# Router and expert gathers on unnormalised token rows, turned rows first in a step, offset expert rows

## The chip, the cores and the metric

The kernel runs on one core of one Trainium2 chip. The metric is the device time of one launch in microseconds (us). The engines are PE (TensorE), DVE (VectorE), ACT (ScalarE), POOL (GpSimd) and SP (SyncE, which here only issues DMAs).

## The reference, cut to what matters

A first block (latent attention and a gated embedding) feeds a second one: gated delta rule and retention, an output product, and a mixture of 64 experts of which every token uses two. All is float32, with 1024 tokens of 1024 numbers. What the change touches is the end of the second block:

```python
x = x + jnp.einsum("bse,ed->bsd", mixed, w_out[l])
h2 = rms_norm(x, ffn_norm[l])          # x * rsqrt(mean(x*x) + EPS) * w
x = x + hierarchical_moe(h2, w_router_group[l], w_router_expert[l], w_gate[l], w_up[l], w_down[l])
...
g_logits = hf @ w_router_group         # 8 groups: the largest
e_logits = hf @ w_router_expert        # 64 experts: the best two of that group
xs = ht[tok]                           # token rows sorted by expert
gate = lax.ragged_dot(xs, w_gate, group_sizes)
up = lax.ragged_dot(xs, w_up, group_sizes)
y = lax.ragged_dot((jax.nn.silu(gate) * up).astype(xs.dtype), w_down, group_sizes)
```

## The kernel before

**The second block** handles 8 tiles of 128 tokens in steps. In step s the pieces named `n_` (new tile) work on tile s, `o_` (the states and outputs) on s - 1, `e_` (the output product, eight pieces `e_p0` to `e_p7`, and `e_x0`, `e_x1`, which add its two halves to the token rows `res`) on s - 2, `l_` (norm, turns, router logits) and `r_` (routing) on s - 3, `z_` (the expert table) on s - 4. The order of the pieces in a step is written out by hand in the list ORDER, with lists of their own in ENDING for steps T = 8, 9, 10 and 11; each engine runs the pieces that it has in that order. Steps 3 to 7 have all pieces and are alike. The eight PSUM banks are given out from the same lists: `n_` and `o_` jobs rotate over three banks each, the others have a home. H0 and H1 (the turned rows), M1 and OUT1 (the second half of the output product) live in bank 7, OUT0, M0, LG (logits), RK (rank) and TB (table) in bank 6; in the steps from T on H0 and H1 have banks 0 and 1. `begin` makes PE wait until the bank's last reader has let go of it.

For a tile, `l_sq` squares the rows on ACT (into `hn`, as a place to throw them), `l_rs` makes the scale on POOL, `l_hn` writes the normalised rows `hn` on DVE with a stride, `l_turn0` and `l_turn1` turn them on PE (four 128x128 blocks each) and copy them on ACT to `hn_t`, `l_logits` multiplies them with `w_r`, and ACT stores `hn` to `hn_d` in DRAM. `r_max` to `r_top2` choose experts on DVE (some twenty small operations from the first `r_one` to `r_m`), `r_rank` counts the tokens ahead in each expert on PE, `r_place` and `r_rows` work out the slots, `z_table` and `z_keep` sum them to a table, from whose last state `src_i`, the list for the gathers, is made. A piece named `q_` is the `r_` piece of the tile before. `x_10`, `x_40`, `x_48` are idle turns on PE that fill a wait.

**The experts** run in 32 pairs. A pair holds 128 slots, 64 for each of its two experts, filled from slot 0 of each half. POOL gathers the rows (`rows`, three buffers) by an indirect DMA from `hn_d`; PE turns them (`turn_rows`, L2890), ACT and DVE copy a half each (`half_rows`, L2962), PE makes the gate and up products (L2901), ACT and DVE silu and product, PE turns that and multiplies with the down weights (L2919), and POOL scatters the rows to `y_d`. The weights, 6.3 MB a pair, have three buffers and come on SP's queue. Pairs 0 to 2 are issued in the last steps; the gate and up weights of pair p + 3 when PE has made those products of pair p. At the end the token rows and the two rows of `y_d` of each token are added and normalised.

Of the kernel before, what the change touches and what calls it, by code (L numbers as in the profile page):

```python
# [32 lines left out]
N_BLOCKS = 2 * S // HB + EXPERTS - 1  # L33
# [6 lines left out]
for _name, _n in (("ident", P), ("tri", P), ("ones", P), ("inv", ROPE // 2), ("levels", 6 * HB), ("ident64", HB), ("decay", BH * P),  # L40
                  ("qdec", BH), ("kdec", BH), ("gend", BH), ("iota", P), ("neghalf", 8), ("before", P), ("asg", 2 * T), ("pcol", 1),
                  ("first", GROUPS), ("limit", EXPERTS)):
    CONST[_name] = (_at, _n)
    _at += _n
# [4 lines left out]
def constants():  # L49
# [27 lines left out]
    put("limit", HB + HB * (np.arange(EXPERTS)[None, :] % 2))  # L77
    ang = np.arange(S, dtype=np.float32)[:, None] * (10000.0 ** (-np.arange(0, HD, 2) / HD)).astype(np.float32)[None, :]
# [19 lines left out]
def build(nc, A, out):  # L98

    ctx = ExitStack()  # L100
    with ctx:  # L101
# [1838 lines left out]
        hn_d = dram("hn_d", (S, D))  # L1940
# [5 lines left out]
        ss_x4, ms_x4, rs_x4 = col(48, 1), col(49, 1), col(50, 1)  # L1946
# [5 lines left out]
        class Count:  # L1952
# [12 lines left out]
            def wait(self, eng, name, t):  # L1965
                if not isinstance(t, int) or t >= 0:
# [23 lines left out]
        ENDING = {T: ("l_sq o_read z_table z_keep o_turn l_rs o_new e_turn o_scores o_out l_hn e_p0 o_mix l_turn0 l_turn1 o_state o_sq e_p1 e_x0 "  # L1990
                      "l_logits e_p2 e_p3 r_max r_group o_end e_p4 e_p5 e_p6 e_p7 r_top1 r_top2 e_x1 r_rank r_place r_rows").split(),
                  T + 1: "e_turn l_sq l_rs z_table z_keep e_p0 l_hn e_p1 e_x0 e_p2 e_p3 e_p4 e_p5 e_p6 e_p7 e_x1 l_turn0 l_turn1 l_logits".split(),
                  T + 2: ("l_sq l_rs l_hn l_turn0 l_turn1 q_max q_group q_top1 q_top2 x_10 p_logits x_10 q_rank q_place q_rows z_table x_40 r_max z_keep r_group r_top1 r_top2 "
                          "r_rank x_10 r_place r_rows").split(),
                  T + 3: "z_table x_48 z_keep".split()}
        LAG = {"a": -1, "n": 0, "o": 1, "e": 2, "l": 3, "r": 3, "p": 3, "d": 3, "q": 4, "z": 4, "x": 4}
# [7 lines left out]
                  "e_p2": "OUT1", "l_turn0": "H0", "l_turn1": "H1", "l_logits": "LG", "p_logits": "LG", "r_rank": "RK", "q_rank": "RK", "z_table": "TB"}  # L2004
# [8 lines left out]
        for s in STEPS:  # L2013
            for name in ENDING.get(s, ORDER):
                t = s - LAG[name[0]]
                if 0 <= t < T:
                    for job in BEGINS.get(name, "").split():
                        if job in HOME:
                            b = HOME[job] if s < T else HOME_END[job] + (job == "LG" and t == T - 1)
# [39 lines left out]
        pool_l = Count("l_pool", "ms rs"); act_l = Count("l_act", "sq"); dve_l = Count("l_dve", "hn")  # L2059
# [4 lines left out]
        def d0_sp(sp):  # L2064
# [10 lines left out]
            sp.dma_start(fg_row[:, :], A["ffn_norm_2"][0].partition_broadcast(P)).then_inc(s_fg, 16)  # L2075
            sp.dma_start(w_r[:, :, 0:GROUPS], A["w_router_group_2"][0].rearrange("(p k) n -> p k n", p=P)).then_inc(s_wr, 16)
            sp.dma_start(w_r[:, :, GROUPS:], A["w_router_expert_2"][0].rearrange("(p k) n -> p k n", p=P)).then_inc(s_wr, 16)
            products_over(sp)
            load_tk(sp, 1)
            sp.dma_start(w_o2[:, :, :], A["w_out_2"][0].rearrange("(k p) n -> p k n", p=P)).then_inc(s_wo2, 16)  # L2080

# [1312 lines left out]
```

## Time and profile before

| | us |
|---|---|
| median of 3 runs | 2111.21 (2109.64 to 2113.0) |
| the profiled execution | 2114.67, its span 2112.9 |
| PE busy over the span | 1949.3 (92%), granted clock 0.969 |
| DVE, ACT, POOL busy | 794.8, 615.1, 600.9 |
| DMA moved | 371.80 MB, mean 176 GB/s |

The page gives shares over the whole span, in which many stages with different limits lie behind each other. The first block ends at about 1187 us, the steps of the second run to about 1565, the experts to about 2073, the closing sums to the end. In the page's 40 slices the DMA share is under 0.7 in every slice up to about 1585 and 0.9 or more in nearly all behind it.

### The profile page before, as it was taken

The page shows a single profiled execution, that of the slowest core. Times are in us where ns is not written, and L with a number is a line of the kernel's source. Part 1 is how long each engine was busy: PE and PEld are TensorE (multiplying, and loading weights), DVE is VectorE, ACT ScalarE, POOL GpSimd, SP SyncE. Part 2 cuts the span into 40 slices and gives each one's busy share as a digit, 9 for nine tenths or more (in the row PEclk, how much of TensorE's full clock was granted, in tenths as well). Part 3 has the DMA queues.
Part 4 walks back from the last instruction along what each step waited for, and adds up shares of the span by engine and source line. Part 5 has one row for each costly group of instructions (what it writes and reads, how often), then busy time and mean ns, then how long its engine had stood idle before and what let it go on. Part 6 is the DMA issues. An engine that isn't in the chain of part 4 may idle for free. (4 is left out here: it accounts for less than half of the span.)

```text
span 2112.9 us, 31128 instructions
## 1 busy us (share of the span) xinstructions
PE 1949.3 (92%) x12049; PEld 1376.3 (65%) x12049; DVE 794.8 (38%) x1445; ACT 615.1 (29%) x1324; POOL 600.9 (28%) x611
## 2 busy tenths in 40 slices
PE   8999999999999989999999899999979888878785
PEld 7998887787787766878887767677653223323222
DVE  5223246666453443441112356666531211111114
ACT  5233145555333442332122333232212111111111
POOL 1225387342120110001003576765211111111102
PEclk9999999999999999999999999999999999999998
DMA  5103461211320253622333422311669999999996
GB/s 209 52 31 139 137 214 27 51 26 46 140 92 21 50 111 67 91 60 86 104 105 106 165 76 81 100 62 56 244 247 420 424 425 424 424 424 422 420 389 271
DMA packets 101730, 371.80 MB, mean 176 GB/s; under 512 B 17429, under 2 KB 40154, under 8 KB 74714
## 3 DMA queue, kind: packets, MB, share of 16 engines
q1 hardware_dynamic: 82592, 323.55, 42.7%
q0 software_dynamic: 16704, 42.10, 5.1%
q10 hardware_dynamic: 2298, 4.23, 0.5%
q8 instruction: 98, 1.61, 0.3%
q14 instruction: 38, 0.31, 0.0%
HBM read 321.47 MB, written 65.14 MB: 183 GB/s over the span
## 5 line engine op out<-in xcount | busy, mean ns | idle before, releaser
L2901 PE MATMUL ps<-w_gu,rows_t 128*64 128x512 f32 x1024 | 257.8, 662 | 57.1 <-DMA w_gu<-w_up 55.5
L2901 PEld LDWEIGHTS ps<-w_gu,rows_t 128*64 128x64 f32 x1024 | 78.7, 151 | 212.9 <-issue 153.7
L3165 POOL DMA_INDIRECT y_d<-y_out,asg_i x32 | 32.1, 1003 | 426.5 <-DVE y_out L2985 400.5
L2976 DVE TENSOR_TENSOR act_s<-act_g,ps 128x256 f32<-128x256 f32 x32 | 13.5, 421 | 321.0 <-ACT act_g L2967 321.0
L2333 PE MATMUL ps<-w_o,mix_t 128*128 128x512 f32 x256 | 122.6, 609 | 0.0
L2919 PE MATMUL ps<-w_d,act_tt 128*64 128x512 f32 x512 | 116.9, 598 | 0.5 <-DMA w_d<-w_down 0.5
L1120 ACT ACTIVATE prob<-ps,stats 128x1024 f32<-128x1024 f32 (+7 forms) x128 | 94.4, 737 | 62.2 <-DVE stats L1083 61.8
L2967 ACT ACTIVATE act_g<-ps 128x256 f32<-128x256 f32 x32 | 12.3, 383 | 320.1 <-PE ps L2901 320.1
L310 PE MATMUL ps<-tk_lo,h_hi 128*128 128x512 f32 x256 | 100.4, 392 | 3.0 <-DVE tk_lo L302 3.0
L310 PE MATMUL ps<-tk_hi,h_hi 128*128 128x512 f32 x256 | 100.3, 392 | 0.0
L310 PE MATMUL ps<-tk_hi,h_lo 128*128 128x512 f32 x256 | 100.2, 391 | 0.0
L1083 DVE TENSOR_REDUCE stats<-ps 128x1 f32<-128x1024 f32 (+7 forms) x128 | 97.0, 758 | 4.4
L482 PE MATMUL ps<-w_u_lo,x_hi 128*128 128x444 f32 (+2 forms) x256 | 92.8, 363 | 5.6 <-DVE x_lo L302 3.6
L998 PE MATMUL ps<-consts,prob 128*128 128x128 f32 x576 | 89.3, 277 | 6.8 <-DVE prob_t L1057 5.4
L482 PE MATMUL ps<-w_u_hi,x_lo 128*128 128x444 f32 (+2 forms) x256 | 92.1, 360 | 0.0
L482 PE MATMUL ps<-w_u_hi,x_hi 128*128 128x444 f32 (+2 forms) x256 | 91.8, 359 | 0.0
L829 POOL TENSOR_SCALAR stats<-stats 128x1 f32<-128x1 f32 (+1 forms) x40 | 8.3, 207 | 278.1 <-ACT junk_b L1392 102.7
L310 PE MATMUL ps<-h_lo,ch_hi 128*128 128x512 f32 x192 | 77.9, 406 | 8.9 <-DVE ch_lo L302 5.6
L998 PEld LDWEIGHTS ps<-consts,prob 128*128 128x128 f32 x576 | 65.8, 140 | 20.0 <-ACT prob L1120 9.2
L1013 PE MATMUL ps<-prob_t,v_all 128*64 128x128 f32 x1152 | 77.0, 278 | 0.9 <-DVE prob_t L1057 0.9
L310 PE MATMUL ps<-k_lo,q_hi 96*128 96x512 f32 (+2 forms) x192 | 76.8, 400 | 1.1 <-ACTq L1124 1.1
L310 PE MATMUL ps<-h_hi,ch_lo 128*128 128x512 f32 x192 | 76.6, 399 | 0.0
(481 smaller groups left out, 4362.9 us busy)
## 6 DMA issues: line engine op xcount, KB each, us to landing
w_gu<-w_gate SPq DMA_DIRECT2D x64, 1024.0 KB, 22.9
w_gu<-w_up SPq DMA_DIRECT2D x64, 1024.0 KB, 26.5
w_d<-w_down SPq DMA_DIRECT2D x64, 1024.0 KB, 25.2
w_tk<-w_in SPq DMA_DIRECT2D x5, 2048.0 KB, 12.7
proj_d<-tok_o POOLq DMA_DIRECT2D x40, 256.0 KB, 2.3
tk_in<-proj_d SPq DMA_DIRECT2D x8, 1280.0 KB, 6.0
w_ch<-w_in SPq DMA_DIRECT2D x12, 512.0 KB, 9.5
proj_d<-conv_o POOLq DMA_DIRECT2D x12, 512.0 KB, 3.9
```

The lines of the kernel that those rows point to most:

```text
L310: mm = pe.matmul(out_, a, b_, start=(n == 0), stop=(n == 3 * len(pairs) - 1))
L482: mm = pe.matmul(b[:, 0:U_COLS[g][1]], a[:, k, :], w[:, k, :], start=(n == 0), stop=(n == 3 * KD - 1))
L998: mm = pe.transpose(b[:, (k - 4 * g) * P:(k - 4 * g + 1) * P], prob[j % 2][:, k * P:(k + 1) * P], ident)
L1013: mm = pe.matmul(ps[half, b, (i % 4) * P:(i % 4 + 1) * P], v_all[:, k, bass.ds(u * (2 * VD) + a * VD, VD)], prob_t[(2 * x + a) % 4][:, k, ...
L1083: v.tensor_reduce(nmax[j % 4], flat[:, 0:n], AX.X, ALU.max, negate=True).then_inc(s_max, 1)
L1120: act.activation(prob[j % 2][:, 0:n], flat[:, 0:n], ACT.Exp, bias=nmax[j % 4], accum_out=rsum[p][:, row(j), j % 2:j % 2 + 1]).then_inc(s_e ...
L2333: mm = pe.matmul(b, mix_t[:, k, :], w_o2[:, k, j * BANK:(j + 1) * BANK], start=(k == 0), stop=(k == KD - 1))
L2901: mm = pe.matmul(ps[half, 2, :].rearrange("p (g n) -> p g n", g=2), rows_t[:, k, half], w_gu[q][:, h, :, k, :], start=(k == 0), stop=(k == ...
L2919: mm = pe.matmul(ps[half, 4 + j, :], act_tt[:, k, half], w_d[q][:, h, k, j * BANK:(j + 1) * BANK], start=(k == 0), stop=(k == 1))
L2967: act.activation(act_g[:, :], ps[:, 2, 0:DE], ACT.Silu).then_inc(s_actg, 1)
L2976: v.tensor_tensor(act_s[:, :].rearrange("q (k p) -> q k p", k=2), by_k(act_g[:, :]), by_k(ps[:, 2, DE:]), ALU.mult).then_inc(s_acts, 1)
L3165: pool.indirect_dma_start(out=y_d, out_offset=bass.IndirectOffsetOnAxis(ap=idx, axis=0), in_=y_out[q][:, :], in_offset=None, bounds_check= ...
```

## The change

1. The router and the gathers take the token rows as they are. The norm's gain goes into the router's weights once (`l_gain`, on DVE) and into the copies of the experts' turned rows (`half_rows`: four ACT operations with a scale, and a product on DVE). The scale of a token goes into the softmax of the routing and, for a slot, is worked out again from the gathered row (`row_squares` on ACT, `row_scales` on POOL) and applied in silu and product. `l_hn`, `hn`, `hn_d` and its stores go; the gathers read `x4_d`, to which the rows `res` were stored before too.
2. The order lists: `l_turn0` and `l_turn1` stand first in a step; in the last steps the routing of tile 6 stands among the output products, so that one routing stands behind the last product.
3. The wait for the cleared states moves from PE's first piece of the steps to `o_read` of tile 0. The loads of the gains and of `w_r` stand behind `w_o2` on SP's queue; `w_r` and the weights' blocks take row k * 128 + p or p * 8 + k to suit, so the gathered rows are turned with a stride of 8 elements.
4. Each expert's slots begin (e // 2) % 8 rows into its half (`TURN`, `start`).

```diff
+TURN = 8
-N_BLOCKS = 2 * S // HB + EXPERTS - 1
+N_BLOCKS = EXPERTS + 2 * S // (HB + 2 - TURN)
...
+    put("start", (NOWHERE * (np.arange(EXPERTS)[None, :] % 2) + np.arange(EXPERTS)[None, :] // 2 % TURN) / P)
...
-        ORDER = ("l_sq n_turn n_decay o_read l_rs n_scores l_hn e_turn o_new e_p0 n_first l_turn0 o_out l_turn1 e_p1 e_x0 n_y1 "
+        ORDER = ("l_turn0 l_turn1 n_turn n_decay o_read l_sq l_gain l_rs n_scores e_turn o_new e_p0 n_first o_out e_p1 e_x0 n_y1 "
...
-                  T + 1: "e_turn l_sq l_rs z_table z_keep e_p0 l_hn e_p1 e_x0 e_p2 e_p3 e_p4 e_p5 e_p6 e_p7 e_x1 l_turn0 l_turn1 l_logits".split(),
+                  T + 1: ("l_turn0 l_turn1 e_turn l_sq l_rs l_logits e_p0 z_table z_keep r_max r_group e_p1 e_x0 r_top1 r_top2 e_p2 e_p3 r_rank e_p4 r_place "
+                          "r_rows e_p5 e_p6 e_p7 e_x1").split(),
+                  T + 2: "l_turn0 z_table l_turn1 x_10 l_logits z_keep l_sq l_rs r_max x_40 r_group r_top1 r_top2 r_rank x_10 r_place r_rows".split(),
...
-            sp.dma_start(fg_row[:, :], A["ffn_norm_2"][0].partition_broadcast(P)).then_inc(s_fg, 16)
...
+            sp.dma_start(gain_kp[:, :], A["ffn_norm_2"].rearrange("a (k p) -> p (a k)", p=P), allow_slow_non_contiguous=True).then_inc(s_fg, 16)
+            sp.dma_start(gain_pk[:, :], A["ffn_norm_2"].rearrange("a (p k) -> p (a k)", p=P)).then_inc(s_fg, 16)
...
+                if t == 0:
+                    pe.wait_ge(s_zero, 4)
...
-                    dve_l.wait(pe, "hn", t)
-                    turn4(f"H{j}", t, q4(hn[:, j * BANK:(j + 1) * BANK]))
+                    copied(pe, f"OUT{j}", t)
+                    turn4(f"H{j}", t, q4(res2[t % 2][:, j * BANK:(j + 1) * BANK]))
...
+            by_k = rows[q][:, :].rearrange("q (p k) -> q k p", k=KD)
...
-                    mm = pe.transpose(ps[:, j, k * P:(k + 1) * P], rows[q][:, (4 * j + k) * P:(4 * j + k + 1) * P], ident)
+                    mm = pe.transpose(ps[:, j, k * P:(k + 1) * P], by_k[:, 4 * j + k, :], ident)
...
-            ins = eng.activation(dst, ps[:, 0, :], ACT.Copy) if j == 0 else eng.tensor_copy(dst, ps[:, 1, :])
+            if j == 0:
+                for k in range(4):
+                    ins = eng.activation(rows_t[:, k, :], ps[:, 0, k * P:(k + 1) * P], ACT.Copy, scale=gain_pk[:, k:k + 1])
+            else:
+                ins = eng.tensor_tensor(rows_t[:, 4:8, :], q4(ps[:, 1, :]), bc(gain_pk[:, 4:8], P), ALU.mult)
...
+            act.activation(sq_out[:, :], rows[q][:, :], ACT.Square, scale=D ** -0.5, accum_out=ss_c[:, c:c + 1]).then_inc(s_csq, 1)
```

**The start of a step on PE** (here step 3; the names in brackets are the semaphores that a row waits for). Before, the new tile's turns follow the last output products at once:

```order
L2333 MATMUL ps<-w_o_240,mix_t 128x512 x2
L2215 MATMUL ps<-consts,qk_n 128x128 [waits bank_free0,d_dve_ahead]
L2215 MATMUL ps<-consts,qk_n 128x128 x3
L2215 MATMUL ps<-consts,qk_n 128x128 [waits bank_free1]
L2215 MATMUL ps<-consts,qk_n 128x128 x3
L2226 MATMUL ps<-tri_g,consts 128x512 [waits bank_free2,d_pool_ahead]
```

In the changed kernel both halves of the token rows stand between them:

```order
L2344 MATMUL ps<-w_o_240,mix_t 128x512 x2
L2224 MATMUL ps<-consts,res_0_245 128x128 [waits bank_free7,bank_free6]
L2224 MATMUL ps<-consts,res_0_245 128x128 x3
L2224 MATMUL ps<-consts,res_0_245 128x128 [waits bank_free7]
L2224 MATMUL ps<-consts,res_0_245 128x128 x3
L2224 MATMUL ps<-consts,qk_n 128x128 [waits bank_free0,d_dve_ahead]
```

Both of the new pieces wait for bank 7, the first for the addition of the output product's second half, the second for the copy of the first.

**Step 9 on PE**, from the last rank products before it to its last output products. L2333 and L2344 are output products, L2350 and L2362 logits, L2355 with L2360 and L2367 with L2372 rank products, L2365 with L2366 and L2377 with L2378 table products. Before:

```order
L2333 MATMUL ps<-w_o_240,mix_t 128x512 x8
L2355 MATMUL ps<-r_m,consts 128x64
L2360 MATMUL ps<-r_sum,consts 128x64
L2215 MATMUL ps<-consts,mixed 128x128 x8
L2365 MATMUL ps<-ohb_283,ohs_281 128x32
L2366 MATMUL ps<-ohb_284,ohs_282 128x32
L2333 MATMUL ps<-w_o_240,mix_t 128x512 x16
```

In the changed kernel:

```order
L2224 MATMUL ps<-consts,res_0_245 128x128 x8
L2224 MATMUL ps<-consts,mixed 128x128 x8
L2362 MATMUL ps<-w_r,xr_t 128x72 x8
L2344 MATMUL ps<-w_o_240,mix_t 128x512 x4
L2377 MATMUL ps<-ohb_288,ohs_286 128x32
L2378 MATMUL ps<-ohb_289,ohs_287 128x32
L2344 MATMUL ps<-w_o_240,mix_t 128x512 x6
L2367 MATMUL ps<-r_m,consts 128x64
L2372 MATMUL ps<-r_sum,consts 128x64
L2344 MATMUL ps<-w_o_240,mix_t 128x512 x6
```

The turns of tile 6 (`res_0_245`), its logits and its rank products now stand inside the step; they stood behind the output products.

**Behind the last output product on PE** (L155 and L160 are the idle turns). Before:

```order
L2215 MATMUL ps<-consts,hn 128x128 x8
L2350 MATMUL ps<-w_r,hn_t 128x72 x8
L2215 MATMUL ps<-consts,hn 128x128 x8
L155 MATMUL ps<-consts 128x128 x10
L2350 MATMUL ps<-w_r,hn_t 128x72 x8
L155 MATMUL ps<-consts 128x128 x10
L2355 MATMUL ps<-r_m,consts 128x64
L2360 MATMUL ps<-r_sum,consts 128x64
L2365 MATMUL ps<-ohb_283,ohs_281 128x32
L2366 MATMUL ps<-ohb_284,ohs_282 128x32
L155 MATMUL ps<-consts 128x128 x40
L2355 MATMUL ps<-r_m,consts 128x64
```

In the changed kernel:

```order
L2224 MATMUL ps<-consts,res_1_246 128x128 x4
L2377 MATMUL ps<-ohb_288,ohs_286 128x32
L2378 MATMUL ps<-ohb_289,ohs_287 128x32
L2224 MATMUL ps<-consts,res_1_246 128x128 x4
L160 MATMUL ps<-consts 128x128 x10
L2362 MATMUL ps<-w_r,xr_t 128x72 x8
L160 MATMUL ps<-consts 128x128 x40
L2367 MATMUL ps<-r_m,consts 128x64
L2372 MATMUL ps<-r_sum,consts 128x64
L160 MATMUL ps<-consts 128x128 x10
```

One set of logits and one of rank products stand there in place of two each.

## Rows read from the trace of the kernel before

**Rows 1.** Windows of five steps of the second block: sum and mean of the busy time.
```profile
sum 222.60, PE 216.09 PEld 157.41 DVE 146.68 ACT 70.17 POOL 146.03; mean PE 43.22 PEld 31.48 DVE 29.34 ACT 14.03 POOL 29.21
```

**Rows 2.** Windows: length, busy time (instructions) of each engine, granted clock, DMA share, GB/s.
```profile
1570.00:1580.00 10.00, 8.63 (x44) 3.69 (x42) 1.80 (x3) 2.98 (x5) 0.99 (x1) 1.00 0.31 80
...
1700.00:1800.00 100.00, 82.83 (x364) 29.60 (x362) 13.59 (x31) 11.85 (x25) 12.10 (x12) 0.91 1.01 425
```

**Rows 3.** Timeline of SP's queue: start, length, issue of a load.
```profile
1535.35 0.75 SPq L2834 DMA_DIRECT2D w_gu<-w_gate  x1
...
1578.28 0.33 SPq L2834 DMA_DIRECT2D w_gu<-w_gate  x1
```

**Rows 4.** Timeline of PE: start, length, instructions [idle before <- releaser].
```profile
1544.35 1.97 PE L2215 MATMUL ps<-consts,hn 128*128 128x128 f32 x8 [6.61 <-DVE hn L2592]
...
1547.72 1.90 PE L2350 MATMUL ps<-w_r,hn_t 128*128 128x72 f32 x16
...
1549.46 1.26 PE L155 MATMUL ps<-consts 128*128 128x128 f32 x10
...
1559.94 0.33 PE L2355 MATMUL ps<-r_m,consts 128*128 128x64 f32 x2
...
1569.09 1.09 PE L2890 MATMUL ps<-consts,rows 128*128 128x128 f32 x8 [0.28 <-DMA rows<-hn_d,src_i]
...
1571.17 7.09 PE L2901 MATMUL ps<-w_gu,rows_t 128*64 128x512 f32 x32 [0.99 <-DVE rows_t L2962]
```

**Rows 5.** Timeline of ACT, then DVE, behind the last product.
```profile
1540.08 1.06 ACT L2458 ACTIVATE hn<-res 128x1024 f32<-128x1024 f32 x1 [4.41 <-DMA hn_d<-hn]
...
1544.21 0.16 DVE L2605 TENSOR_REDUCE r_one<-ps 128x1 f32<-128x8 f32 x1
...
1553.38 0.17 DVE L2605 TENSOR_REDUCE r_one<-ps 128x1 f32<-128x8 f32 x1
...
1558.68 0.22 DVE L2633 TENSOR_TENSOR r_m<-oh,oh 128x64 f32<-128x64 f32 x1
...
1564.07 0.18 DVE L2661 TENSOR_SCALAR src_i<-asg_i 128x32 int32<-128x32 int32 x1
```

**Rows 6.** Timeline at the end of a step (PE, DVE) and at its turns (PE, ACT).
```profile
1445.26 1.04 PE L2215 MATMUL ps<-consts,qk_n 128*128 128x128 f32 x8
...
1445.56 0.68 DVE L2582 TENSOR_TENSOR res<-ps,res 128x512 f32<-128x512 f32 x1
...
1412.09 0.66 PE L2215 MATMUL ps<-consts,hn 128*128 128x128 f32 x4
...
1412.58 1.06 PE L2209 MATMUL ps<-v_new,attn_t 128*128 128x128 f32 x8
...
1412.78 0.60 ACT L2388 ACTIVATE hn_t<-ps 128x512 f32<-128x512 f32 x1 [4.17 <-PE ps L2215]
```

**Rows 7.** Timeline of PE in step 9.
```profile
1517.01 1.31 PE L2215 MATMUL ps<-consts,mixed 128*128 128x128 f32 x8
...
1519.66 0.41 PE L2365 MATMUL ps<-ohb,ohs 128*128 128x32 f32 x2 [1.34 <-DVE r_sum L2649]
...
1520.13 13.98 PE L2333 MATMUL ps<-w_o,mix_t 128*128 128x512 f32 x32
```

**Rows 8.** Timeline at the beginning of step 1: PE, then ACT.
```profile
1191.27 1.15 PE L2215 MATMUL ps<-consts,qk_n 128*128 128x128 f32 x8 [3.31 <-POOL u_fin L2793]
...
1207.52 2.19 ACT L2449 ACTIVATE w_o<-w_o,gain_ab 128x1024 f32<-128x1024 f32 x2
```

**Rows 9.** A window, and PE's timeline, at the end of the expert stage.
```profile
2048.00:2052.00 4.00, 2.40 (x14) 0.82 (x14) 0.59 (x1) 0.38 (x1) 1.00 (x1) 1.00 0.79 319
...
2061.16 3.65 PE L2919 MATMUL ps<-w_d,act_tt 128*64 128x512 f32 x16 [0.52 <-DMA w_d<-w_down]
```

**Rows 10.** Timeline of PE at an idle gap, and the window behind it.
```profile
1222.42 0.74 PE L2279 MATMUL ps<-y_w,t_w 64*64 64x64 f32 x8 [2.36 <-ACT y_w L2418]
...
1222.90:1226.31 3.41, 2.74 (x13) 2.14 (x11) 2.02 (x2) 1.19 (x2) 3.33 (x4) 0.50 0.87 291
```

More of the change, by code:

```diff
@@ L41 @@
                   ("qdec", BH), ("kdec", BH), ("gend", BH), ("iota", P), ("neghalf", 8), ("before", P), ("asg", 2 * T), ("pcol", 1),
-                  ("first", GROUPS), ("limit", EXPERTS)):
+                  ("first", GROUPS), ("limit", EXPERTS), ("start", EXPERTS)):
     CONST[_name] = (_at, _n)
@@ L2018, in build @@
                         if job in HOME:
-                            b = HOME[job] if s < T else HOME_END[job] + (job == "LG" and t == T - 1)
+                            b = (HOME if s < T else HOME_END)[job]
                         else:
@@ L2097, in d_sp @@
                         loaded(sp, s_x4st, t - 2)
-                        dve_l.wait(sp, "hn", t - 2)
+                        full(sp, "H1", t - 2)
+                        act_l.wait(sp, "sq", t - 2)
                     sp.dma_start(res2[t % 2][:, :], x1_d[t * P:(t + 1) * P, :]).then_inc(s_res2[t % 2], 16)
@@ L2454, in l_sq @@
                 copied(act, "OUT1", t)
-                if t > 0:
-                    loaded(act, s_hnst, t - 1)
-                    full(act, "H1", t - 1)
-                act_l.done(act.activation(hn[:, :], res2[t % 2][:, :], ACT.Square, accum_out=ss_x4), "sq")
+                act_l.wait(act, "sq", t - 1)
+                act_l.done(act.activation(sq_out[:, :], res2[t % 2][:, :], ACT.Square, accum_out=ss_x4[:, t:t + 1]), "sq")
             def l_turn(j):
                 def piece(t):
-                    copy(f"H{j}", t, hn_t[:, 4 * j:4 * j + 4, :])
-                    if j == 0:
-                        dve_l.wait(act, "hn", t)
-                        act.dma_start(hn_d[t * P:(t + 1) * P, :], hn[:, :]).then_inc(s_hnst[t % 2], 16)
+                    copy(f"H{j}", t, xr_t[:, 4 * j:4 * j + 4, :])
                 return piece
@@ L2469, in r_group @@
                 dve_r.wait(act, "gd", t)
-                act_r.done(act.activation(r_ge[:, :], r_gd[:, :], ACT.Exp, accum_out=keep("gsum", t)), "exp")
+                pool_l.wait(act, "rs", t)
+                act_r.done(act.activation(r_ge[:, :], r_gd[:, :], ACT.Exp, scale=r_rs[:, t:t + 1], accum_out=keep("gsum", t)), "exp")
             pieces = dict(a_sums=a_sums, n_turn=n_turn, n_scores=n_scores, o_new=o_new, o_turn=o_turn, o_sq=o_sq, e_turn=e_turn,
-                          l_sq=l_sq, l_turn0=l_turn(0), l_turn1=l_turn(1), r_group=r_group, q_group=r_group)
+                          l_sq=l_sq, l_turn0=l_turn(0), l_turn1=l_turn(1), r_group=r_group)
             for s in range(1, LEV):
@@ L3181, in moe_pool @@
                 gather(src_i[:, p:p + 1], p)
+            for p in range(2):
+                row_scales(pool, p, p)
             for p in range(1, N_FIX):
```

136 lines of the change are left out of this document (80 added, 56 removed).

## The prediction

> **What bounds the kernel now.** I read the busy shares by time first, then the idle time of TensorE (PE) with its releasers, then the chain behind the last product of the second block.
>
> Two stretches set the end. The steps of the second block are bound by PE: in five of them PE works 216.09 of 222.60 us, 43.2 of every 44.5 [rows 1]. Then the expert stage is bound by DMA. Its transfers take 0.31 of the DMA engines in 1570 to 1580, and 1.01 of them at 425 GB/s in 1700 to 1800, where PE has 82.8 us of work in 100 [rows 2]. The stream starts when SP issues the gate and up weights of pair 3, at 1578.28, since there are three weight buffers and that load waits for the products of pair 0; pair 2 had gone out at 1535.35 [rows 3]. Those products begin at 1571.17 [rows 4]. Between the two the DMA queues run dry. So whatever moves "load of pair 3" moves the end by as much, and what the stream itself takes is added. Everything else on the other engines is cover.
>
> What puts pair 3 there: the last product ends at 1534.11 (v from here on) [rows 7]. The token rows of tile 7 are squared at 1540.08, because the squares overwrite hn and the store of tile 6 holds it for 4.41 us more; the scaled rows come to PE at 1544.35; then DVE does the whole routing of tile 6 (1544.21 to 1553.38) before that of tile 7, whose gather list is ready at 1564.25, v + 30.1 [rows 4, 5].
>
> **The change, part by part** (plus is later; the sum is made against the profiled 2114.67 us, its span 2112.9; the median of the runs is 2111.21, 3.5 lower, and I carry differences over unchanged).
>
> *Turned rows first in a step.* H0, H1 and the second half of the product all live in PSUM bank 7. Now H0 stands directly behind the last product and must wait until DVE has added that half. In a row of before, the next PE work begins at 1445.26 and DVE's addition runs from 1445.56 to 1446.24; with 0.15 for the handover PE would stand 1.13 us [rows 6]. H1 waits for H0's copy, which starts 0.69 after the turn and takes 0.60; the turn itself holds PE 0.49, and with 0.1 for the handover it stands 0.9 more [rows 6]. Before, both turns lay inside the step behind other work, with no idle time. Added: 2.03 us in each of the five steps 3 to 7, 10.2. In steps 8 and 9 the two have banks of their own, and only H1 waits for the addition (1.13 less H0's 0.45): 0.7 in step 8, and the same inside step 9's term.
>
> *Step 9.* Before: from 1517.01 to v, 17.1 us, with 1.34 of waiting for the table row of tile 5 [rows 7]. That wait goes (the table products come behind four products of the output). In come both turns of tile 6 (0.49 each) with 0.7 of waiting, its logits (1.9 [rows 4]), its rank products (0.4), and a wait of 2.0 for the choice of tile 6. DVE took 5.5 us from the maximum to the end of r_m for tile 7 (1553.38 to 1558.90) [rows 5], with one operation on the way that ran long; I take 5.3. Ahead of it stand the table products, behind four output products of 0.87 (32 in 13.98 on the trace, two each [rows 7]), and the table's row, 5.0 us after the logits; among it one addition of 0.7; so r_m comes 11.0 us after the logits, while PE has ten output products and the table's, 9.1. Sum: 1.0 + 0.7 + 1.9 + 0.4 + 2.0 - 1.34 = 4.7.
>
> *Step 1.* PE waited 3.31 us for POOL's clearing of the states at 1191.27 [rows 8]. The wait now stands behind the turns and the decay product, which takes up to 2.6 of it; but the product weights land for ACT only at 1207.52 whatever PE does [rows 8], and ACT is behind until 1222. I take 1.2 off (0 to 2.6). The smaller gain loads go on SP's queue between the product weights and the rows of tile 2, in place of a 512 KB load; their many small pieces could hold tile 2's rows by 3 to 4 us, which have 7 us of cover before ACT asks for them.
>
> So v comes 10.2 + 0.7 + 4.7 - 1.2 = 14.4 later.
>
> *Behind the last product.* Now: H0 at v, H1 at v + 1.13, copied by v + 2.5; ten idle turns (1.26 [rows 4]) end at v + 2.8, logits 1.9, so the maximum starts at v + 4.8; choice 5.3, v + 10.1; the forty idle turns take 5.0 at full clock and end before that, v + 9.8. From the rank products to the list is 1559.94 to 1564.25, 4.3 [rows 4, 5]: the list is ready at v + 14.5, in place of v + 30.1: -15.6. What went: the store's 4.41 and the squares, their scale and the scaled rows (1540.08 to 1544.35), and one routing of 9.2. The squares, their scale and the store of the rows still run, behind the logits, and are done long before the list.
>
> *What is late next.* The gathers now start about 1 behind the list, at v + 15.5, while pair 2, issued 1.2 behind v, is still in flight: which by its 6.3 MB at 425 GB/s and what is queued ahead of it lasts to about v + 22. From the list (1564.25) to the turns of the first gather's rows took 4.8 us [rows 4, 5], half of it in flight; beside the weights that half could double: 0 to +2.4, I take +1.5. The first pair's copy becomes four on ACT (about 1.1, starting 0.44 ahead of DVE's 0.69): +0.1 at most.
>
> *Expert stage.* The four scaled copies, the squares (1.06 [rows 5] and 0.19) and POOL's two small operations hide behind the 7.1 us of gate and up products; PE has 12.1 us of work in a pair of 16 [rows 2]. The turned rows now are read with a stride of eight elements. No row shows PE doing that; the nearest is the contiguous 1.09 a pair [rows 4], and 3.9 us of slack cover up to 4.5 times as much. Price 0 (0 to +20 beyond it, a rival).
>
> *The offsets.* Each expert's rows begin 0 to 7 rows into its half of 64 instead of at row 0. If a DMA engine serves fixed rows, those that serve the first rows of a half carry more than the mean and end the stream late. The trace shows unequal ends: the share falls to 0.79 in 2048 to 2052, yet the last down weights land at 2061.16 [rows 9]. So 13 us at the end belong to some engines alone. The change can take none of it or all: 0 to -13. It shifts starts by up to 7 where halves are on average half full, so it evens out a part; I take the middle, -6.5. The Trainium skill (DMA: Bandwidth & Descriptors, The descriptor swizzle) says that partitions 0 to 3 and 32 to 35 are served by one engine, and so on in fours. An estimate from that page and the token counts of the reference gives the heaviest engine 186 rows of each gather kind before and 164 after, with a mean of 128, which would be about 7 us less; no row here shows the mapping itself.
>
> *Clock.* A PE gap of 2.36 us in front of 1222.42 was followed by a stretch at half clock (0.50, the 1.2 GHz level, [rows 10]); the gaps up to 1 us in the steps were not. The new step start has 2.03 us idle in two pieces with short turns between. I expect one start of five to lose the clock, for half of the 3.4 us of such a stretch: 1.7, +2 (0 to five times that, +8.5, and up to +10 where it lasts longer once). The Trainium skill (TensorE: Matmul & The Clock Gate, Part 4: PE-mode transpose) says that transposes don't count as busy in the way products do. By that rule the turns right behind each gap would count as idle time too, and this term would be nearer +10 than +2. No row parts turns from products, so it stays open.
>
> Sum: 14.4 - 15.6 + 1.5 + 0.1 + 2 - 6.5 = -4.1; the scatter of the last pair and the landing of its last rows lie on more even engines too, for which I take off 0.5 to 1. That makes **-5 us, 2106**.
>
> **The rivals.** A run of this kernel can be told from no change at about 0.2%, 4.2 us.
> - *The order evens out, and the stream gets shorter* (forecast): 2101 to 2109, chance 0.45.
> - *The offsets change nothing.* If engines take rows in turn, all are equally loaded, and the tail of 13 us comes from elsewhere. Then 2106 + 6.5 = 2112.5, 2111 to 2115. Chance 0.20. For it: the x rows are fetched beside the last loads, too. Against it: the share falls well before the last landing [rows 9].
> - *The step starts cost more* (slower side): the places are the five starts where H0 stands behind bank 7. If the clock falls at each, that is +8.5 in place of +2: 2113 with the offsets' 6.5, 2119 without. It decides for slower from 4.3 us a start where the offsets give their 6.5 (9.2 more in five), and from 3.0 where they give nothing; the sum has 2.4. Chance 0.16.
> - *Strided turns make PE the bound* (slower side): over 4.9 us a pair instead of 1.09, PE passes 16 us; at six times, +1.5 in each of 29 pairs, +44, 2150. The first pairs would show it. Chance 0.03.
> - *The order is worth more than the sum says.* If DVE, without the scaled rows in each step, lets PE close some of the 1.3 idle us of a step [rows 1] and the step 1 wait gives its 2.6: 1.4 and up to 5 times 1 less; with the whole 13 of the stream 2093. Chance 0.16.
>
> **How the numbers follow.** The time is the first case's. Faster takes nearly four fifths of the first case (0.35) and the last (0.16): 0.51. Same takes 0.10 of the first, 0.17 of the second and 0.02 of the third: 0.29. Slower: 0.20. The range goes from the last case's half way, 2096, to 2117 in the third; the first case's own range is 2101 to 2109.
>
> **What would show it.** Steps of 46.5 us, each with two gaps of 1.1 and 0.9 at its start and the turns of `res` between them; the end of the last product at about 1548; the gather list 14.5 us behind it; pair 3's load at 1578 to 1581; PE's clock at 1.00 at most step starts; and from that load to the products of the last down weights 476 us in place of 482.9 (1578.28 to 2061.16), with the DMA share higher in the last 12. I am wrong if the load of pair 3 moves by more than 4 us either way, or if that stretch keeps its 483.

## The result, and the profile after

In 14 runs each the changed kernel took 2117.72 us (2113.5 to 2120.63) and the kernel before 2113.11 (2109.64 to 2116.87): ratio 1.0026, 95% interval 1.0018 to 1.0033. By the medians it is 4.6 us slower, where 5 us faster were forecast. One later execution of the kernel before took 4895.69 us and is left out of the ratios below.

The page of the changed kernel, its span and its busy times:

```profile
span 2118.7 us, 31432 instructions
...
PE 1953.2 (92%) x12039; PEld 1375.7 (65%) x12039; DVE 782.7 (37%) x1439; ACT 669.3 (32%) x1484; POOL 620.3 (29%) x675
```

Busy shares tell little, so I laid the profiled executions side by side by their marks. The end of the first block lies up to 5 us apart from one execution to the next, also between kernels that are alike up to there (first turns of the steps, less the idle time before them: 1183.2 to 1188.1 in thirteen traces; 1187.96 in the one of before, 1185.06 in the changed one's), so every mark below is counted from there.

| from the end of the first block to | before | changed | later by |
|---|---|---|---|
| end of step 2 | 79.52 | 78.86 | -0.7 |
| end of step 7 | 301.8 | 315.1 | +13.3 |
| end of step 8 | 329.05 | 344.9 | +15.9 |
| pair 2's load (last product + 1.2) | 347.4 | 367.1 | +19.7 |
| gather list | 376.3 | 381.1 | +4.8 |
| first gathered rows turned | 381.1 | 387.0 | +5.9 |
| pair 3's load | 390.3 | 397.9 | +7.6 |
| last gate and up products | 861.8 | 869.5 | +7.7 |
| end of the span | 924.9 | 933.6 | +8.7 |

The profiled execution of the changed kernel (2120.45) is one of its slower ones; part of that +8.7 is lost clock, which not every execution loses as often. The last +1.0, behind the last gate and up products, is in no term of the sum: that stretch takes 63.2 us in before and 63.5 to 64.5 in the twelve traces of the changed kernel and its variants, and no run shows why.

*The start of a step.* PE's timeline of the changed kernel (start, length, idle before and releaser), and the window behind it, which answer to [rows 6]:

```profile
1401.63 1.98 PE L2344 MATMUL ps<-w_o,mix_t 128*128 128x512 f32 x4
...
1404.58 0.63 PE L2224 MATMUL ps<-consts,res 128*128 128x128 f32 x4 [0.96 <-DVE res L2589]
...
1405.98 0.63 PE L2224 MATMUL ps<-consts,res 128*128 128x128 f32 x4 [0.78 <-ACT xr_t L2399]
...
1406.45 1.45 PE L2224 MATMUL ps<-consts,qk_n 128*128 128x128 f32 x8
...
1405.00:1409.00 4.00, 3.22 (x16) 2.41 (x15) 0.00 (x0) 2.75 (x5) 0.00 (x0) 0.74 0.32 131
```

PE waits 0.96 us for the addition in bank 7, then 0.78 for the copy of the first turns, where 1.13 and 0.9 were forecast. Each such step takes 2.15 us longer than before, where 2.03 were. In this execution the clock falls as well: the turns take 1.45 in place of 1.04, the granted clock of the window is 0.74, and the step is 1.66 longer still. Two of five starts did that here. Over the first four steps, which in before take 177.78 us together, six of the seven traces with the turns at the start show 188.1 to 188.2, and one 186.4, which is 177.78 and four times 2.15: one loss of 1.67 in six of seven.

*The last steps and the tail.* PE's timeline, which answers to [rows 4] and [rows 7]:

```profile
1524.27 0.43 PE L2367 MATMUL ps<-r_m,consts 128*128 128x64 f32 x2 [1.63 <-DVE r_m L2635]
...
1545.02 0.43 PE L2367 MATMUL ps<-r_m,consts 128*128 128x64 f32 x2 [1.66 <-DVE r_m L2635]
...
1550.72 0.60 PE L2224 MATMUL ps<-consts,res 128*128 128x128 f32 x4
...
1552.06 0.63 PE L2224 MATMUL ps<-consts,res 128*128 128x128 f32 x4 [0.37 <-DVE tab L2658]
...
1553.62 1.91 PE L2362 MATMUL ps<-w_r,xr_t 128*128 128x72 f32 x16
...
1561.87 0.44 PE L2367 MATMUL ps<-r_m,consts 128*128 128x64 f32 x2 [1.98 <-DVE r_m L2635]
...
1572.07 1.15 PE L2895 MATMUL ps<-consts,rows 128*128 128x128 f32 x8 [1.33 <-DMA rows<-x_d,src_i]
...
1574.20 8.75 PE L2906 MATMUL ps<-w_gu,rows_t 128*64 128x512 f32 x32 [0.99 <-ACT rows_t L2968]
...
1586.84 8.78 PE L2906 MATMUL ps<-w_gu,rows_t 128*64 128x512 f32 x32 [0.96 <-DVE rows_t L2970]
```

The rank products of steps 8 and 9 both wait for DVE's choice, 1.63 and 1.66 us; the first was not in my sum. The last output product ends as the turns at 1550.72 begin. The last rank products start at 1561.87, and the first gathered rows are turned at 1572.07, 1.33 us after the idle turns have run out. Gate and up products of pairs 0 and 1 then take 8.75 and 8.78 us in place of 7.09, at a granted clock of 0.81 over each: half clock again for a part of them.

### The profile page after: what moved, and what is told of

Read it like the earlier page. It is cut to its first block and busy times, and to the rows that moved or that the text cites. A ratio compares the mean times of both kernels' runs of the same rounds, so it can differ in the third digit from the quotient of the medians.

```text
span 2118.7 us, 31432 instructions
## 1 busy us (share of the span) xinstructions
PE 1953.2 (92%) x12039; PEld 1375.7 (65%) x12039; DVE 782.7 (37%) x1439; ACT 669.3 (32%) x1484; POOL 620.3 (29%) x675
## 5 line engine op out<-in xcount | busy, mean ns | idle before, releaser
L3202 POOL DMA_INDIRECT y_d<-y_out,asg_i x32 | 32.4, 1013 | 384.2 <-DVE y_out L3011 384.2
L3001 DVE SCALAR_TENSOR_TENSOR act_s<-ps,rs_c,act_g 128x256 f32<-128x256 f32 x32 | 15.5, 484 | 328.4 <-ACT act_g L2991 328.4
L2344 PE MATMUL ps<-w_o,mix_t 128*128 128x512 f32 x256 | 123.1, 609 | 0.0
L2991 ACT ACTIVATE act_g<-ps,rs_c 128x256 f32<-128x256 f32 x32 | 15.2, 474 | 277.2 <-PE ps L2906 277.1
## 6 DMA issues: line engine op xcount, KB each, us to landing
w_ch<-w_in SPq DMA_DIRECT2D x12, 512.0 KB, 10.1
```

The costliest lines, as they stand in the source:

```text
L2344: mm = pe.matmul(b, mix_t[:, k, :], w_o2[:, k, j * BANK:(j + 1) * BANK], start=(k == 0), stop=(k == KD - 1))
L2991: act.activation(act_g[:, :], ps[:, 2, 0:DE], ACT.Silu, scale=scale_of(c)).then_inc(s_actg, 1)
L3001: v.scalar_tensor_tensor(act_s[:, :].rearrange("q (k p) -> q k p", k=2), by_k(ps[:, 2, DE:]), scale_of(c), by_k(act_g[:, :]), ALU.mult, AL ...
L3202: pool.indirect_dma_start(out=y_d, out_offset=bass.IndirectOffsetOnAxis(ap=idx, axis=0), in_=y_out[q][:, :], in_offset=None, bounds_check= ...
```

## The experiments

Each kernel was timed beside the kernel before on the same chip and profiled once, so every reading of a trace below is of one execution. Edits are against the changed kernel where nothing else is said. The kernels were timed in three groups on three chips, on which the kernel before had medians of 2112.6, 2112.6 and 2113.7, and the changed kernel itself was timed apart from all three. Where two kernels of different groups are compared, the distance of each from the kernel before beside it is therefore the better measure:

| kernel | us above the kernel before beside it |
|---|---|
| the changed kernel | +4.6 |
| `turns_inside` | -7.6 |
| `turn1` | +7.8 |
| `table_ahead` | +2.8 |
| `idle60` | +3.9 |
| `zeroes_on_act` | +6.8 |
| `routing_behind` | +5.2 |
| `zero_wait_first` | +5.6 |
| `best` | -12.9 |
| `best_zero_first` | -12.6 |
| `best_turn1` | -10.2 |
| `late_down` | -16.6 |

**Turns back inside the step** (`turns_inside`).

```diff
-        ORDER = ("l_turn0 l_turn1 n_turn n_decay ... e_p0 n_first o_out e_p1 e_x0 n_y1 "
+        ORDER = ("n_turn n_decay ... e_p0 n_first l_turn0 o_out l_turn1 e_p1 e_x0 n_y1 "
```

> The changed kernel with the two turn pieces put back inside the step in ORDER (behind n_first and behind o_out), steps 3 to 7 alone. Theory A, the 2.15 us of waiting at each of five step starts and the two losses of the clock there (1.7 each) are added one for one: five steps of 44.5, the last product 10.7 to 14 us earlier, the end 10 to 14 us earlier than the changed kernel. Rival: what is saved there comes back as another wait (the rows' loads, the routing), and the end moves by less than 5.

Measured: 2105.02 us, ratio 0.997 (0.9959 to 0.998), 12.7 under the changed kernel (12.2 by the table). Its PE timeline at a step's end:

```profile
1395.07 1.98 PE L2344 MATMUL ps<-w_o,mix_t 128*128 128x512 f32 x4
...
1396.89 1.04 PE L2224 MATMUL ps<-consts,qk_n 128*128 128x128 f32 x8
```

The next tile's turns follow the products without a gap, the first four steps take 177.81 us, as before, and the clock stays. The stalls (10.75) and one loss of the clock (1.67) are 12.4 us together: they came back one for one. So this one edit turns the change from slower into faster, by 0.3%.

**Offsets off** (`turn1`), `TURN = 8` to `TURN = 1`.

> The changed kernel with every expert's rows begun at row 0 of its half (TURN = 1), nothing else. Theory A, the offsets do even out the DMA engines, and their gain lies hidden behind a starved stretch at the start of the stream: from the load of pair 3 to the start of the last gate and up products 474 to 478 us in place of 471.5, and the whole 2 to 6 us slower than the changed kernel. Theory B, the offsets do nothing: 471.5 again, within 1 us of the changed kernel.

Measured: 2120.46 us, 1.0041 (1.0027 to 1.0055). Pair 3's load and the last gate and up products, first of this run, then the latter of the changed kernel (its load: 1582.98):

```profile
1578.69 0.33 SPq L2838 DMA_DIRECT2D w_gu<-w_gate  x1
...
2053.12 7.09 PE L2906 MATMUL ps<-w_gu,rows_t 128*64 128x512 f32 x32 [0.31 <-DMA w_gu<-w_up]
```

```profile
2054.51 7.09 PE L2906 MATMUL ps<-w_gu,rows_t 128*64 128x512 f32 x32 [0.23 <-DMA w_gu<-w_up]
```

From the one to the other 474.43 us without the offsets, 471.53 with them. The gain grows along the stream, as it would with a load that is unequal between the engines: 0.2 us at pair 8, 1.1 at 16, 2.6 at 24, 2.9 at 31. The whole time moved by 2.7 (3.2 by the table). Theory A holds, with 2.9 us in place of the 6.5 that I took; that the engines' load is what changed is argued, since no view shows the single engines.

**The same where the stream starts without a hole** (`best_turn1`, the kernel `best` below with `TURN = 1`).

> The kernel of the run best with every expert's rows begun at row 0 of its half, nothing else; here neither the starved start of the stream nor a lost clock stands beside the offsets. Theory A, the offsets take about 3 us off the stream whatever lies ahead of it: from the load of pair 3 to the start of the last gate and up products 473 us in place of 470.0, the end 3 us later, 2102.6. Theory B, they had most of their worth hidden in the changed kernel: 476 to 477, the end 6 to 7 later.

Measured: 2103.45 us, 0.9952 (0.9941 to 0.9964), 3.8 above `best` (2.7 by the table). Load and last products of `best`, then of `best_turn1`:

```profile
1567.14 0.33 SPq L2838 DMA_DIRECT2D w_gu<-w_gate  x1
...
2037.13 7.09 PE L2906 MATMUL ps<-w_gu,rows_t 128*64 128x512 f32 x32 [3.21 <-DMA w_gu<-w_up]
```

```profile
1565.46 0.33 SPq L2838 DMA_DIRECT2D w_gu<-w_gate  x1
...
2038.86 7.09 PE L2906 MATMUL ps<-w_gu,rows_t 128*64 128x512 f32 x32 [1.51 <-DMA w_gu<-w_up]
```

469.99 against 473.40: 3.4 us. So the offsets are worth about 3 in both places where they were tried; nothing of 6 was hidden. How far a single trace can be trusted here: with the offsets in, the stretch takes 469.8 to 470.4 in six traces that have pair 1 at full clock, and 471.4 to 471.7 in the four others.

**Silu's table loaded ahead** (`table_ahead`).

```diff
         def moe_act(act):
...
+            act.activation(act_tt[:, 0, 0:1], gain_pk[:, 0:1], ACT.Silu)
             half_rows(act, 0)
             squares(0)
```

> The changed kernel with one silu of a single column on ACT ahead of the first pair's copies, so that ACT's table is loaded there and not between the first gate and up products and the silu. Theory A, the table load of 1.28 us lies on the path to pair 4's load, behind which DMA is starved: pair 4's load 1.3 earlier, the end 1.3 earlier. Rival: pair 4's load is hidden and the end does not move.

Measured: 2115.44 us, 1.0016 (1.0007 to 1.0025), 2.3 under the changed kernel (1.8 by the table, and the two intervals overlap). The stretch in question, in the changed kernel's rows: SP's loads of pairs 2, 3 and 4, ACT's table load, and two windows:

```profile
1552.16 0.43 SPq L2838 DMA_DIRECT2D w_gu<-w_gate  x1
...
1582.98 0.33 SPq L2838 DMA_DIRECT2D w_gu<-w_gate  x1
...
1595.66 0.33 SPq L2838 DMA_DIRECT2D w_gu<-w_gate  x1
...
1583.03 1.28 ACT L2991 ACT_TABLE_LOAD   x1 [8.04 <-PE ps L2906]
...
1594.00:1596.00 2.00, 2.00 (x12) 0.79 (x9) 0.00 (x0) 0.27 (x1) 0.00 (x0) 1.00 0.73 301
...
1596.00:1598.00 2.00, 2.00 (x15) 1.02 (x15) 1.18 (x2) 1.34 (x5) 0.00 (x0) 1.00 0.66 166
```

The table load starts when the first gate and up products are done (before, it ran from 1570.39, ahead of them). It and the lost clock hold pair 1, and pair 4's load comes 12.7 us behind pair 3's. Pair 3's gate and up weights, 4.2 MB, are 9.9 us of stream at 425 GB/s, and the DMA share falls to 0.73 and 0.66. In before pair 4's load came 9.1 behind pair 3's, and the share stayed at 1.0. In `table_ahead`:

```profile
1569.11 7.09 PE L2906 MATMUL ps<-w_gu,rows_t 128*64 128x512 f32 x32 [0.99 <-ACT rows_t L2968]
...
1578.81 7.09 PE L2906 MATMUL ps<-w_gu,rows_t 128*64 128x512 f32 x32 [0.96 <-DVE rows_t L2970]
...
1576.22 0.33 SPq L2838 DMA_DIRECT2D w_gu<-w_gate  x1
...
1585.93 0.33 SPq L2838 DMA_DIRECT2D w_gu<-w_gate  x1
```

The two loads are 9.7 apart. This execution has pairs 0 and 1 at full clock, too, so the 470.36 us from pair 3's load to the last products (1.2 less than in the changed kernel) are the worth of both. The table load alone opened no hole: `idle60` and `routing_behind`, below, keep it between the products and the silu and have both pairs at full clock. There the loads are 11.0 apart (here in `idle60`), the DMA share from 1592 to 1596 in `idle60` stays at 1.00 and 0.98, and the stream takes 469.8 and 470.0 us, no more than here. Theory A's 1.3 us for the table load is not borne out.

```profile
1580.03 0.33 SPq L2838 DMA_DIRECT2D w_gu<-w_gate  x1
...
1591.01 0.33 SPq L2838 DMA_DIRECT2D w_gu<-w_gate  x1
```

**More idle turns ahead of the first rows** (`idle60`), `x_48=idle(48)` to `idle(60)`.

> The changed kernel with 60 idle turns in place of 48 ahead of the first gathered rows, so that PE stands 0.0 instead of 1.3 us there. Theory A, that gap costs the clock in the first two pairs: their products take 7.1 us in place of 8.75 and 8.78, pair 3's load comes 1.7 and pair 4's 3.3 earlier, the end 2 to 3.3 earlier. Rival: the clock falls for the wait for the copies that follows (0.99) all the same, and nothing moves.

Measured: 2116.53 us, 1.0026 (1.0015 to 1.0036), 1.2 under the changed kernel (0.7 by the table). PE's rows:

```profile
1570.87 1.06 PE L2895 MATMUL ps<-consts,rows 128*128 128x128 f32 x8
...
1572.91 7.09 PE L2906 MATMUL ps<-w_gu,rows_t 128*64 128x512 f32 x32 [0.98 <-DVE rows_t L2970]
...
1583.89 7.09 PE L2906 MATMUL ps<-w_gu,rows_t 128*64 128x512 f32 x32 [0.96 <-DVE rows_t L2970]
```

Both pairs run at full clock, as theory A said, and from pair 3's load it takes 469.79 us, 1.7 less than in the changed kernel. Pair 3's load itself gains nothing: it stands 32.4 us behind the start of the last turns, and 32.3 in the changed kernel. The 60 turns end late: from the list to the first rows it takes 7.1 us and not 5.9, and the list is 0.7 later, with ten idle turns ahead of it at half clock (2.34 us in place of 1.26). So full clock in the first pairs is worth 1.7 us of stream. That the 12 added turns kept it is not shown: `turn1` has 48 turns and pair 0 at full clock as well, and `best` has a gap of 1.78 us there and both pairs at full clock. The gain in the time is within the scatter.

**Gather buffers cleared on ACT** (`zeroes_on_act`).

```diff
-                pool.memset(rows[q][:, :], 0.0).then_inc(s_gi, 1)
+                act.activation(rows[q][:, :], consts[:, 0:D], ACT.Copy, scale=0.0).then_inc(s_gi, 1)
```

> The changed kernel with the three gather buffers cleared on ACT (a copy with scale 0) and not by POOL's memset. In the traces one small DVE operation of the last routing takes 0.9 us (before) and 1.75 (after) in place of 0.23 while that memset runs. Theory A, the memset holds DVE: with ACT the operation takes 0.23, the list is 1.5 us earlier, and so is the end. Rival: the long operation has another cause and stays. ACT's clearing ends well before the gathers in either case.

Measured: 2119.36 us, 1.0032 (1.002 to 1.0044): no gain, and by the table 2.2 more than the changed kernel, with intervals that overlap. The changed kernel's DVE and POOL in its last routing:

```profile
1558.16 1.75 DVE L2625 TENSOR_SCALAR r_oh<-r_val,r_one 128x8 f32<-128x8 f32 x1
...
1566.01 0.18 DVE L2663 TENSOR_SCALAR src_i<-asg_i 128x32 int32<-128x32 int32 x1
...
1557.16 2.73 POOL L3212 MEMSET rows<- 128x1024 f32 x3 [1.88 <-DVEq L2618]
```

And this run's DVE, PE and a window:

```profile
1555.11 0.23 DVE L2625 TENSOR_SCALAR r_oh<-r_val,r_one 128x8 f32<-128x8 f32 x1
...
1561.44 0.18 DVE L2663 TENSOR_SCALAR src_i<-asg_i 128x32 int32<-128x32 int32 x1
...
1568.93 1.97 PE L2895 MATMUL ps<-consts,rows 128*128 128x128 f32 x8 [2.76 <-DMA rows<-x_d,src_i]
...
1562.00:1566.00 4.00, 4.00 (x39) 3.93 (x36) 0.00 (x0) 0.00 (x0) 2.79 (x3) 1.00 1.02 430
```

The long operation is gone (0.23 in place of 1.75), the list comes 13.9 us behind the last turns' start (1547.68) and not 15.5, as theory A had it. But the first rows reach PE 21.25 us behind that mark; in the changed kernel it was 21.35. The gathers ran beside the weights of pair 2 at a DMA share of 1.02. That they ended with them is a guess here, which `late_down` tests.

**Routing of tile 6 behind the last product** (`routing_behind`; the last logits also get a bank of their own).

```diff
-                  T + 1: ("... l_logits e_p0 z_table z_keep r_max r_group e_p1 e_x0 r_top1 r_top2 e_p2 e_p3 r_rank e_p4 r_place r_rows e_p5 ..."),
-                  T + 2: "l_turn0 z_table l_turn1 x_10 l_logits z_keep l_sq l_rs r_max ..."
+                  T + 1: "... l_logits e_p0 z_table z_keep e_p1 e_x0 e_p2 e_p3 e_p4 e_p5 ...",
+                  T + 2: "l_turn0 l_turn1 q_max q_group q_top1 q_top2 x_10 p_logits l_sq l_rs x_10 q_rank q_place q_rows z_table x_40 r_max ..."
```

> The changed kernel with the routing of tile 6 alone put back behind the last product (its turns and logits stay in step 9). Theory A, the order of the last steps pays: step 9 is 2 us shorter, but the gather list comes 20.5 us behind the last product in place of 15.3, the end 3 us later, about 2121. Rival: the gain behind the last product was all in the normalised rows (store, squares, scale), and taking the routing out of step 9 gains its 2 us and costs nothing: 2116.

Measured: 2117.73 us, 1.0022 (1.0013 to 1.0032), the changed kernel's own time. Its last turns and its first rows on PE:

```profile
1548.22 0.60 PE L2224 MATMUL ps<-consts,res 128*128 128x128 f32 x4
...
1572.73 1.16 PE L2896 MATMUL ps<-consts,rows 128*128 128x128 f32 x8 [0.47 <-DMA rows<-x_d,src_i]
```

Step 9 is 2.5 us shorter, the list 4.0 us later behind it (19.5 in place of 15.5), but the rows only 3.2: from the list to the rows it takes 5.0 us and not 5.9, presumably because the weights let go of the DMA engines meanwhile. The net is 0.7 us at the rows: the routing moved in among the products is worth next to nothing here. Neither theory had it quite: the rival's time, by another reason.

**The wait for the cleared states first** (`zero_wait_first`, and `best_zero_first` on top of `best`).

```diff
             d_begin(pe, pieces, dict(own, gc=lambda: d0_pe(pe)))
+            pe.wait_ge(s_zero, 4)
             d_steps(pe, pieces)
```

> The changed kernel with PE's wait for the cleared states put back ahead of the first piece of the steps. Theory A, the moved wait is what brought the start of step 3 3.6 to 3.9 us forward: the turns of the first new tile start at about 1191 again, the start of step 3 and the end come 3 to 4 us later than in the changed kernel, about 2121. Rival: ACT and the landing of the output weights set those steps, the gain in the trace came with the smaller loads, and the end moves by under 1.5.

> The kernel of the run best with PE's wait for the cleared states put back ahead of the first piece of the steps. With the turns inside the steps no clock is lost at their starts, so that the runs scatter less than those of zero_wait_first. Theory A: the start of step 3 and the end 3.5 to 4 us later, 2103.3. Rival: under 1.5 later, as the medians of zero_wait_first had it.

Measured: 2118.13 us, 1.0032 (1.002 to 1.0044), and 2101.07, 0.9945 (0.9932 to 0.9957): 0.4 and 1.4 above the kernels without the edit (1.0 and 0.3 by the table), both within the intervals. Counted from the end of the first block, step 3's new turns start at 79.52 us in `best_zero_first` and at 77.4 to 79.0 in its four kin, at 82.50 against 80.4 to 82.0 in the others. The rival holds: the moved wait is worth 0.8 to 1 us. The 3.6 to 3.9 that I wrote down came from marks not counted from the first block's end.

**All of it together** (`best`): turns inside, silu's table ahead, 58 idle turns, buffers cleared on ACT, and in the lists of steps 8 and 9 `r_rank` behind `e_p4`.

> The changed kernel with four edits together: the turns inside the steps, silu's table loaded ahead and 58 idle turns ahead of the first rows, the gather buffers cleared on ACT, and the rank products of tiles 5 and 6 one output product piece later. From the runs so far: -12.7 for the turns, -1.2 and -1.7 for the starved start of the stream (not quite additive), -1.5 for the clearing, -1 to -3 for the rank products: 2099 to 2103, 10 to 14 under the kernel before. If the stalls only change places: 2105, as with the turns alone.

Measured: 2099.63 us, 0.994 (0.9926 to 0.9953), within the 2099 to 2103 expected. The parts did not all pay. Against `turns_inside`, steps 8 and 9 are 0.86 us shorter each (the rank products), the list is 1.5 us nearer to the last turns (the clearing), but the first rows come 21.4 us behind them in both; the stream is 1.7 us shorter, with pair 1 at full clock.

**Pair 2's down weights behind the gathers** (`late_down`, on top of `best`, 48 idle turns).

```diff
             full(sp, "OUT1", T - 1)
-            load_pair(sp, 2)
+            load_gu(sp, 2)
...
         def moe_sp(sp):
...
+            for q in range(NB):
+                sp.wait_ge(s_gath[q], 16)
+            load_d(sp, 2)
```

> The kernel of the run best with the down weights of pair 2 (2.1 MB, about 5 us of the DMA engines) issued behind the first three gathers and not ahead of them, and 48 idle turns again. In every run of the changed kernel the first rows came to PE 21.1 to 21.3 us behind the last product, whether the list was ready at 13.8 or at 15.3. Theory A, the gathers are served beside pair 2's weights and end with them: now the rows come 18 to 19 us behind the last product, pair 3's load 2 to 3 us earlier, the end as much, 2097. Rival: the gathers have 4.8 us of their own from the list and the weights are no part of it: rows at 21 again, or the idle DMA time only moves and the end stays at 2099.6.

Measured: 2097.06 us, 0.9921 (0.9908 to 0.9933), the fastest of all. Last turns and first rows on PE, the loads of pair 2's down and pair 3's gate weights, and a window:

```profile
1533.46 0.60 PE L2224 MATMUL ps<-consts,res 128*128 128x128 f32 x4
...
1552.36 1.15 PE L2898 MATMUL ps<-consts,rows 128*128 128x128 f32 x8 [0.41 <-DMA rows<-x_d,src_i]
...
1556.08 0.80 SPq L2842 DMA_DIRECT2D w_d<-w_down  x2
...
1561.61 0.33 SPq L2838 DMA_DIRECT2D w_gu<-w_gate  x1
...
1549.00:1552.00 3.00, 2.95 (x28) 2.71 (x25) 0.00 (x0) 0.00 (x0) 2.39 (x3) 1.00 0.46 107
```

The rows come 18.9 us behind the last turns' start in place of 21.4 in `best`, with the list at 13.95 in both, and the DMA share beside the gathers is 0.46. Pair 3's load comes 2.5 us earlier behind those turns, and the stream behind it takes 470.2 us as before. So from a list at 13.95 on, what held the rows was the DMA engines and not the routing. In the changed kernel, with its list at 15.5, the DMA engines can have held them by about 1 us: from the list to the rows it takes 5.9 us there, 4.9 here and 4.8 in before.

## Why the prediction was wrong

- **What bounds the kernel**: held, though +7.6 for the load of pair 3 and +7.7 for the last products agree so closely by luck, since what the stream lost and gained cancelled. Better evidence is that over all traces pair 3's load lies 378 to 399 us behind the first block, and the stream behind it takes 469.8 to 474.4.
- **Turned rows first in a step**, 10.2 forecast, with 2 for the clock: 10.75 for the waits (5 x 2.15), right, and 3.3 of clock in this trace, with one loss of 1.67 in the first four steps of six traces of seven. Taking these turns away again gave back 12.7 us. The rival with its place here, "the step starts cost more", was not reached by these steps alone, at some 2.5 to 2.8 us a start where it asked for 4.3, or 3.0 without the offsets.
- **Step 8**, 0.7 forecast: 2.6. The rank products' wait of 1.63 on DVE, which I had for step 9, arises in step 8 by the same interleaving, and I hadn't looked. **Step 9**, 4.7 forecast: 3.8.
- **Step 1**, -1.2 forecast: -0.7.
- **Behind the last product**, -15.6 forecast: -14.9, the long DVE operation being 1.75. **Gathers**, +1.5: +1.0.
- **First pairs**, +0.1 forecast: pair 0's products at half clock put 1.67 on pair 3's load (as in two of the eleven other variants; what decides it is not shown).
- **The step that failed most is the offsets**, -6.5 as the middle of 0 to -13, with 0.5 to 1 more for the scatter. They measured -2.9 and -3.4. I read the end row [rows 9] as the last down weights' landing; but the last gate and up products and the last down products are 11.4 us apart in both traces, with the same 0.52 us of "waiting" before the latter. In before that wait is the time that ACT takes to copy the turned activations:

```profile
2049.75 7.09 PE L2901 MATMUL ps<-w_gu,rows_t 128*64 128x512 f32 x32 [1.60 <-DMA w_gu<-w_up]
...
2060.68 0.38 ACT L2971 ACTIVATE act_tt<-ps 128x256 f32<-128x256 f32 x1 [1.42 <-PE ps L2909]
```

  The copy ends at 2061.06, and the products start at 2061.16. So that row gave no landing, and the bound of 13 was not one. The page's list of the partitions of each engine (the Trainium skill, DMA: Bandwidth & Descriptors, The descriptor swizzle) led me to an estimate of 7 by the 22 rows fewer on the heaviest engine, counted in both directions. In one direction alone they would be 3.5, by that estimate; no run here parts gather from scatter.
- **And the stream started with a hole**, not in the sum at all: at equal offsets (`turn1`), pair 8 of the changed kernel starts 3.0 us later behind pair 3's load than before, and the last pair 3.0. About 1 of it is the hole (1.4 in the traces with the offsets in): pair 4's load waits for silu's table and the half clock together. With the hole closed the offsets-free kernel (`best_turn1`) still needs 1.9 more than before (473.40 against 471.47), all of it ahead of pair 8. A part has a likely reason: pair 3's gather, 0.52 MB. POOL issued it 7.3 us ahead of pair 3's load before, at a DMA share of 0.47 (1571 to 1574); in the changed kernel it stands in POOL's program behind the scales of pair 1 and comes 5.5 us behind that load (4.3 in `best_turn1`):

```profile
1570.95 0.99 POOL L3160 DMA_INDIRECT rows<-hn_d,src_i  x1 [1.94 <-PE ps L2890]
```

```profile
1588.50 1.12 POOL L3197 DMA_INDIRECT rows<-x_d,src_i  x1 [0.20 <-issue]
```

  At 425 GB/s that is 1.2 us of stream more, by estimate. No run moves this gather, and the rest stays open.

Together, at pair 3's load +7.6 stood against a forecast of 14.4 - 15.6 + 1.5 + 0.1 + 2 = +2.4: 3.0 of the difference is clock, 2.2 the order. Behind it the stream came out at 0 in place of -7, and the closing stretch at +1.0. Had only the size of the offsets been off, the time would have been about 2109.5, so the offsets alone don't explain why it came out slower: the stream's start, the clock and step 8, each put too low or at nothing, did the rest. By the signs that the prediction named for itself it was wrong twice: pair 3's load moved by 4.7 us (1578.28 to 1582.98), and from there to the last down products it took 482.9 us, as before, and not 476. The waits at the step starts, the largest cost by far, had been priced nearly right; it was the rest that turned faster into slower.

The Trainium skill's rule that transposes don't count as busy in the way that products do (TensorE: Matmul & The Clock Gate, Part 4: PE-mode transpose), which I named and priced at nearer +10, was borne out in part: the clock did fall at step starts that hold little but turns and gaps of 0.96 and 0.78, though at one or two of five and not at each. No run parts the turns from the gaps.

The strided turns cost 1.15 us in place of 1.09 a pair: that rival is out.

## What to carry to other kernels

An operation put "first in a step" stands behind whatever the step before frees last; look up its bank and the bank's last reader before its place. When a stage's list is ready earlier, ask what holds the DMA engines at that moment: 2.1 MB of weights not needed yet (4.9 us at 425 GB/s) held the first rows by 2.5 us, while a whole routing taken off the path was worth 0.7. Before a wait "for a DMA" is read as its landing, look at what else the engine needed there: here a copy on ACT ended 0.1 us before the products began.

## What the runs showed of the hardware that was not expected

- A DVE operation of 0.23 us took 0.88 us (before) and 1.75 (changed) while POOL cleared 128x3072 numbers (2.7 us), and 0.23 when ACT did the clearing.
- ACT's table load of 1.28 us ran ahead of the first gate and up products before (at 1570.39) and behind them in the changed kernel (at 1583.03), where a wait on POOL's scale had been added ahead of that silu. That this wait moved it is argued.
- Gate and up products that take 7.09 us at full clock took 8.4 to 10.1 where the clock was at half for part of them. Of the first two pairs it hit both, only the second or neither, from one trace to another; a gap of 1.78 us ahead of the rows' turns was followed by full clock (`best`), and one of 1.33 by half clock (the changed kernel).
- The clock fell at one or two of five otherwise alike step starts, with idle gaps of 0.96 and 0.78 us around short turns, in six traces of seven, and cost about 1.7 us each time; the same four steps without those gaps took 177.8 us in before and in the five variants with the turns inside.
